# Expert stages of a decoder layer on one core: where expert rows and their fetches stand among the half blocks, and the order around the first value block

## The chip, the cores and the metric

One core of one Trainium2 chip. The metric is the device time of the whole kernel in microseconds (us), median of several runs. Engines: PE (TensorE, matmuls; PEld its weight loads), DVE (VectorE), ACT (ScalarE), POOL (GpSimd), SP (SyncE, issues most DMAs). HBM is the chip's memory, SBUF and PSUM the on-chip ones; PSUM has 8 banks of 512 float32 per partition.

## The reference, cut to what matters

The layer is a token mixer (two attention kinds) and then PEER, a channel mixer that picks 16 of 16384 experts per head and token. 16 meta tokens and 256 tokens; the width is 2048.

```
q = (t @ w_query).reshape(n_tok, 8, 2, 64)
s = einsum('thcd,hcnd->thcn', q, sub_keys)
v1, i1 = top_k(s[:, :, 0], 16);  v2, i2 = top_k(s[:, :, 1], 16)
best, j = top_k(v1[..., :, None] + v2[..., None, :], 16)     # over 256 sums
e_idx = i1[j // 16] * 128 + i2[j % 16];  gate = softmax(best)
a = gelu(einsum('cd,chkd->chk', t, expert_u[e_idx]))
out = einsum('chk,chkd->cd', gate * a, expert_v[e_idx])
```

## The kernel before, in words

The first part (norms, projections, attention, output, query) is not touched. It ends about 780 us after the start. Two expert stages follow, each with 128 blocks of 128 experts; a block of the tables is 1 MB. The first 192 tokens (TD) are computed densely: every expert is multiplied, and a table of gates, zero where an expert was not picked, weights the results. The last 64 tokens (TS) are computed from fetched rows: 8 heads x 16 experts for 64 tokens, 128 partitions at a time, are 64 fetches (ROWS) of `u` and later 64 of `v`, 1 MB each.

All products are float32 made from two parts: ACT rounds the 1 MB block to its high part (L457, `hi_block`), DVE subtracts to get the low part (L466/L468, `lo_block`), PE multiplies both. Time is counted in half blocks: DVE calls `step(m)` twice per block, and each step carries what the plan puts there.

**The u stage** (`expert_block`, 128 times). PE does 16 matmuls of 384 columns with the high part (L856) and 16 of 192 with the low part (L861), into bank 0, 1, 2 or 3 in turn. ACT copies half the bank out (L1221), DVE adds the other half for two blocks at once (`expert_sums`, L1777) and so frees the banks. In its steps DVE also does the routing (top 16 of each head, L1674 to L1714) and the products of fetched rows with the token (`row_product`, L1721, the tokens being in banks 4 to 7). The functions `row_at(n)`, `gather_at(n)` and `scatter_at(k)` say at which half block row n is used, and in which place of POOL's instruction order the fetch of row n and scatter k stand. POOL has no clock: it runs its instructions one after another, and waits only for what an instruction needs. Its list has 64 fetches (L1313) and 192 scatters of gates to the HBM table (L1318). There are 3 row buffers (RING), so the fetch of row n waits until row n-3 is used. After the last scatter POOL waits until all scatters are in HBM (L1351), then loads the gates of the first four blocks (L1353).

**SP** issues the load of block n+3 when the low part of block n is done: 3 buffers for the 1 MB blocks.

**The value stage** (`value_block`, 128 times, L879). 20 matmuls of 512 columns a block: 4 with the high part of the gated weights for the first 128 tokens (`part(0, j)`), 4 with their low part `Wlo`, 4 with `Wboth` for the other 64 (`part(1, j)`, banks 4 to 7), and 8 with the low part of the block. `part(0, 0)` writes banks 0 and 1, `part(0, 1)` banks 2 and 3. The weights come by a chain: DVE gates them (`gate_weights`, L1766), ACT rounds them (`weight_hi`, L1210 and L1211, once the block before the last is done on PE), DVE subtracts (`weight_lo`, L1771). DVE also sums the fetched `v` rows (`row_sum`, L1735), one in 3.7 half blocks.

Before, the first value block starts with a wait for banks 0 and 1, two matmuls, and a wait for the sum of the last two u blocks (banks 2 and 3), which DVE does for both at once after PE has ended block 127.

Of the kernel before, what the change touches and what calls it, by code (L numbers as in the profile page):

```python
# [29 lines left out]
ALU = mybir.AluOpType  # L30
# [3 lines left out]
P = 128  # L34
# [10 lines left out]
TD = 192  # L45
# [3 lines left out]
RING = 3  # L49
# [7 lines left out]
B_BRANCH, B_OUT, B_QUERY, B_U, B_V = KC, KC, HEADS, NK, NK  # L57
# [3 lines left out]
F_U = F_QUERY + B_QUERY  # L61
F_V = F_U + B_U
# [104 lines left out]
def hybrid_layer(nc, stream, u_cols, u_rows, v_rows, x_t, params, consts, h1_rows, gates_at, cum_at, out):  # L167
    with ExitStack() as ctx:
# [3 lines left out]
        def sem(name):  # L172
            return ctx.enter_context(nc.semaphore(name))
# [10 lines left out]
        psum = ctx.enter_context(nc.psum_tensor("psum", [P, 8 * 512], F32))  # L184

        def bank(b, a=0, w=512):
            return psum[:, b * 512 + a:b * 512 + a + w]
# [134 lines left out]
        W = arena[:, 0:NK * TD].rearrange("p (c t) -> p c t", c=NK)  # L322
# [12 lines left out]
        Whi = [xr[:, a:a + TD] for a in W_AT]  # L335
        Wlo = [xr[:, a + TD:a + 2 * TD] for a in W_AT]
        Wagain = [xr[:, a + 2 * TD:a + 2 * TD + TS] for a in W_AT]
        Wboth = [xr[:, a + TD + P:a + 2 * TD + TS] for a in W_AT]
# [6 lines left out]
        BEFORE = 12  # L345
# [4 lines left out]

        def row_at(n):
            if n < 46:
                return 6 + n * 9 // 2
            if n < ROWS:
                return 211 + (n - 46) * 5 // 2
            return 2 * B_U + 8 + (n - ROWS) * (2 * B_V - 20) // ROWS

        def gather_at(n):
            return max(row_at(n) - 8, row_at(n - RING) + 1) if n >= RING else -BEFORE

        def scatter_at(k):
            return k * 250 // (ROWS + NSEL) - 2
# [15 lines left out]
        U_BANKS = (0, 1, 2, 3)  # L378
# [5 lines left out]
        def f(ap):  # L384
            return ap.bitcast(F32)
# [4 lines left out]
        hi_done, lo_done, half_done = sem("hi_done"), sem("lo_done"), sem("half_multiplied")  # L390
        bank_free, upper_done = sem("bank_free"), sem("upper_products")
# [30 lines left out]
        low_part = sem("x_lo_products")  # L422
# [152 lines left out]
        def _(pe):  # L575
# [296 lines left out]
            def value_block(base, c, first, idle=None, residual=None):  # L872
                q = c % 2
                hi_w = whi[:, q * D:(q + 1) * D]

                def part(b, j, at, weights, low_part, begin, end):
                    for n in range(2):
                        src = lows[q][:, j, n * 512:(n + 1) * 512] if low_part else hi_w[:, (2 * j + n) * 512:(2 * j + n + 1) * 512]
                        last = mm(at[:, (b * 4 + j * 2 + n) * 512:(b * 4 + j * 2 + n + 1) * 512], weights, src,  # L879
                                  start=begin, stop=end, skip_group_check=True)  # L880
                    return last

                pe.wait_ge(w_hi, base + c + 1)
                pe.wait_ge(hi_done, base * 2 + 2 * F_V + 2 * c + 2)
                if first:
                    pe.wait_ge(bank_free, F_V)
                part(0, 0, psum, Whi[q][:, 0:P], False, first, False)
                if first:
                    pe.wait_ge(bank_free, 2 + F_V)
                part(0, 1, psum, Whi[q][:, 0:P], False, first, False)  # L890
                pe.wait_ge(w_lo, base + c + 1)
                if first:
                    pe.wait_ge(row_used, ROWS)
                if residual is None:
                    for j in range(2):
                        part(0, j, psum, Wlo[q][:, 0:P], False, False, False)
                        part(1, j, psum, Wboth[q], False, first, False)
                else:
                    part(0, 0, psum, Wlo[q][:, 0:P], False, False, False)
                    part(0, 1, psum, Wlo[q][:, 0:P], False, False, False)  # L900
                    part(1, 1 - residual, psum, Wboth[q], False, False, False)
                    pe.wait_ge(low_residual, residual + 1)
                    part(1, residual, psum, Wboth[q], False, False, False)
                pe.wait_ge(lo_done, base * 2 + 2 * F_V + 2 * c + 2)
                for j in range(2):
                    last = part(1, j, psum[0:TS, :], Whi[q][:, P:TD], True, False, True)
                    if j == idle:
                        last.then_inc(low_bank_idle, 1)
                for j in range(2):
                    part(0, j, psum, Whi[q][:, 0:P], True, False, True).then_inc(half_done, 1)  # L910

            value_block(0, 0, True)
            value_block(0, 1, False)
            with pe.Fori(0, B_V // 2 - 4) as i:
                for q in range(2):
# [444 lines left out]
        def _(dve):  # L1360
            V = nc.vector
# [266 lines left out]
            for k in range(KC):  # L1628
                q = k % 2
# [86 lines left out]
            def row_product(n):  # L1716
                s = row_buffer(n)
                if n == 0:
                    dve.wait_ge(x_rows_ps, 1)
                dve.wait_ge(row_in[s], row_loads(n))  # L1720
                V.tensor_tensor_reduce(out=got[s], in0=x_rows, in1=got[s], scale=1.0, scalar=0.0, op0=ALU.mult,  # L1721
                                       op1=ALU.add, accum_out=dots[:, n:n + 1]).then_inc(row_used, 1)
# [14 lines left out]
            def step(m):  # L1737
                for t, k in ROUTE_STEPS.get(m, ()):
                    route(t, k)
                if m in GATE_STEPS:  # L1740
                    route(GATE_STEPS[m], 8)
                if m in ROW_STEPS:
                    n = ROW_STEPS[m]
                    if n < ROWS:
                        row_product(n)
                    else:
                        row_sum(n)

            dve.nop().then_inc(sc_taken, 1)
            for k in range(2 * B_QUERY):  # L1750
# [3 lines left out]
                if k % 2:  # L1754
                    q = k // 2
# [4 lines left out]
            def gate_weights(chunk):  # L1760
                n, q = chunk // 2 % 2, chunk % 2
                if chunk < 4:
                    dve.wait_ge(first_gates[n], 16)
                else:
                    dve.wait_ge(gates_in[n], 16 * (chunk // 4))
                V.tensor_tensor(W[:, chunk, :], W[:, chunk, :], gate_in[n][:, q * TD:(q + 1) * TD], ALU.mult).then_inc(scaled, 1)  # L1766

            def weight_lo(chunk):
                q = chunk % 2
                dve.wait_ge(w_hi, chunk + 1)  # L1770
                V.tensor_tensor(Wlo[q], W[:, chunk, :], f(Whi[q]), ALU.subtract).then_inc(w_lo, 1)  # L1771

            def expert_sums(n):
                dve.wait_ge(half_done, 2 * F_U + 2 * n + 4)
                dve.wait_ge(low_part, n + 2)
                both = psum[:, U_BANKS[n % 4] * 512:(U_BANKS[n % 4] + 2) * 512].rearrange("p (b t) -> p b t", b=2)
                V.tensor_tensor(W[:, n:n + 2, :], both[:, :, 0:TD], W[:, n:n + 2, :], ALU.add).then_inc(bank_free, 2)  # L1777

            for n in range(B_U):
                if n and n % 2 == 0:  # L1780
                    expert_sums(n - 2)
                step(2 * n)
                step(2 * n + 1)
                if n < B_U - 1:
                    lo_block(dve, n + 1)
                if n == B_U - 2:
                    gate_weights(0)
            weight_lo(0)
            expert_sums(B_U - 2)
            lo_block(dve, B_U)  # L1790
            gate_weights(1)
            def bank_residual(n):
# [3 lines left out]

            for c in range(B_V):
                n = B_U + c
                step(2 * n)
                if c < B_V - 2:  # L1800
                    gate_weights(c + 2)
                step(2 * n + 1)
                if c == B_V - 2:
                    bank_residual(0)
                if c < B_V - 1:
                    weight_lo(c + 1)
                if c < B_V - 2:
                    lo_block(dve, n + 1)
                if c == B_V - 2:
                    for z in range(2):  # L1810
                        last_lo_half(dve, z)
                if c in (B_V - 5, B_V - 4):
                    half = slice((c - B_V + 5) * HALF, (c - B_V + 6) * HALF)
                    rows_at = psum[0:TS, 2048 + half.start:2048 + half.stop]
                    dve.wait_ge(rows_back[1], 16)
                    dve.wait_ge(low_bank_idle, c - B_V + 6)
                    V.tensor_tensor(rows_at, rows_at, h1_high[0:TS, half], ALU.add).then_inc(low_residual, 1)
                if c == B_V - 6:
                    dve.wait_ge(acc_moved, 16)
                    V.tensor_tensor(res[TS:P, :], res[TS:P, :], acc[TS:P, :], ALU.add).then_inc(sparse_out, 1)  # L1820
# [81 lines left out]
```

## Time and profile before

| | us |
|---|---|
| median of 3 runs | 1981.13 (1979.11 to 1982.59) |
| the profiled execution | 1977.39 |
| its span, first to last instruction | 1975.5 |
| PE busy | 1950.1 (99% of the span) |
| DVE busy | 1682.3 (85%) |
| ACT busy | 1120.6 (57%) |
| POOL busy | 726.9 (37%), almost all of it in the u stage |

TensorE's granted clock was 0.999 over the span. A PE row counts as busy while its matmuls are in flight, so the share says that PE had work nearly all the time; the gaps between blocks show in the timeline and in the sums over stretches. The two expert stages together run from 781.9 us to the end, 60% of the span.

### The profile page before, as it was taken

The numbers are of one execution on the slowest core, as the hardware profiler recorded it, in microseconds if no ns is written. First come the engines' busy times: TensorE is split into PE (matmuls) and PEld (weight loads), VectorE is DVE, ScalarE is ACT, GpSimd is POOL, SyncE is SP. The second block draws the span as 40 slices with busy tenths as digits, with TensorE's granted clock in tenths as the row PEclk, the third lists the DMA queues.
The fourth block names the chain that finished last, engine by engine and source line by source line (L and its number), as shares of the span: only waits on it lengthen the run. The fifth ranks groups of instructions, "written<-read, shape, count | busy, mean of one in ns | idle before, by whom it ended". The sixth has DMA issues, their size and how long they took to land. (4 is left out here: it accounts for less than half of the span.)

```text
span 1975.5 us, 32460 instructions
## 1 busy us (share of the span) xinstructions
PE 1950.1 (99%) x11696; PEld 1734.8 (88%) x11696; DVE 1682.3 (85%) x2366; ACT 1120.6 (57%) x1585; POOL 726.9 (37%) x406
## 2 busy tenths in 40 slices
PE   8999999999999999999999999999999999999999
PEld 7899989998888888999999999999777777777776
DVE  6877778776878777999999999989888888888897
ACT  7565556555676455666565655645555555555454
POOL 0301110111000001888888888886222232222220
PEclk9999999999999999999999999999999999999999
DMA  5756654566455556999999999999999999999997
GB/s 215 255 168 197 196 191 161 190 202 199 152 175 187 182 188 224 323 312 328 320 323 337 331 307 335 326 383 404 343 379 379 363 374 383 378 375 376 371 385 256
DMA packets 137574, 566.48 MB, mean 287 GB/s; under 512 B 44008, under 2 KB 52080, under 8 KB 88112
## 3 DMA queue, kind: packets, MB, share of 16 engines
q1 hardware_dynamic: 87456, 415.09, 58.5%
q0 software_dynamic: 49776, 148.44, 22.2%
q10 hardware_dynamic: 288, 2.36, 0.3%
q8 instruction: 17, 0.28, 0.1%
q14 instruction: 37, 0.30, 0.0%
HBM read 548.30 MB, written 16.88 MB: 286 GB/s over the span
## 5 line engine op out<-in xcount | busy, mean ns | idle before, releaser
L451 DVE TENSOR_TENSOR wlo<-raw,whi 128x1024 fp32r<-128x1024 f32 x242 | 295.9, 1231 | 112.4 <-PE psum L606 72.1
L856 PE MATMUL psum<-xr,whi 128*128 128x384 f32 x2048 | 381.0, 337 | 2.1 <-ACT whi L457 2.1
L879 PE MATMUL psum<-whi,xr 128*128 128x512 f32 x1512 | 364.0, 389 | 0.8 <-DVE arena L1777 0.6
L856 PEld LDWEIGHTS psum<-xr,whi 128*128 128x128 f32 x2048 | 351.1, 188 | 2.9 <-ACT whi L457 2.6
L602 PE MATMUL psum<-xr,whi 128*128 128x512 f32 x1312 | 336.1, 398 | 5.1 <-issue 3.7
L879 PEld LDWEIGHTS psum<-whi,xr 128*128 128x128 f32 x1512 | 283.4, 188 | 62.4 <-DVE arena L1777 1.1
L457 ACT ACTIVATE whi<-raw 128x2048 fp32r<-128x2048 f32 x168 | 320.8, 1910 | 27.3 <-DMA raw<-v_rows 14.2
L444 ACT ACTIVATE whi<-raw 128x1024 fp32r<-128x1024 f32 x244 | 249.9, 1053 | 101.3 <-DMA raw<-stream 44.2
L1313 POOL DMA_INDIRECT arena<-v_rows,small x64 | 143.8, 2246 | 400.2 <-DVE arena L1735 397.9
L602 PEld LDWEIGHTS psum<-xr,whi 128*128 128x128 f32 x1312 | 236.1, 189 | 50.7 <-issue 4.4
L1318 POOL DMA_INDIRECT gates<-arena x96 | 219.9, 2290 | 29.3 <-issue 28.9
L1318 POOL DMA_INDIRECT gates<-small x96 | 197.3, 2055 | 29.3 <-issue 29.0
L468 DVE TENSOR_TENSOR wlo<-raw,whi 128x2048 fp32r<-128x2048 f32 x76 | 173.8, 2287 | 26.3 <-issue 25.8
L1210 ACT ACTIVATE xr<-arena 128x192 fp32r<-128x192 f32 x128 | 46.7, 365 | 260.4 <-PE psum L879 256.7
L606 PEld LDWEIGHTS psum<-xr,wlo 128*128 128x128 f32 x1312 | 177.9, 189 | 13.8
L1313 POOL DMA_INDIRECT arena<-u_rows,small x64 | 92.3, 1442 | 260.5 <-DMA small<-arena 240.9
L468 DVE TENSOR_TENSOR xr<-raw,whi 128x2048 fp32r<-128x2048 f32 x77 | 176.2, 2289 | 12.4 <-issue 11.4
L606 PE MATMUL psum<-xr,wlo 128*128 128x256 f32 x1312 | 181.8, 281 | 0.0
L1303 POOL TENSOR_TENSOR arena<-arena 128x256 f32<-128x256 f32 x32 | 23.7, 741 | 416.9 <-DVE arena L1450 416.9
L457 ACT ACTIVATE whi<-arena 128x2048 fp32r<-128x2048 f32 x85 | 162.3, 1910 | 15.9 <-DMA arena<-u_cols 9.9
L1221 ACT ACTIVATE arena<-psum 128x192 f32<-128x192 f32 x128 | 42.5, 332 | 222.4 <-PE psum L861 222.4
L1721 DVE CUSTOM_DVE_ANT_0 arena<-psum,arena 128x2048 f32<-128x2048 f32 x64 | 146.2, 2284 | 12.5 <-DMA arena<-u_rows,small 11.7
(276 smaller groups left out, 3232.2 us busy)
## 6 DMA issues: line engine op xcount, KB each, us to landing
raw<-stream SPq DMA_DIRECT2D x244, 512.0 KB, 3.3
raw<-v_rows SPq DMA_DIRECT2D x85, 1024.0 KB, 7.6
raw<-u_cols SPq DMA_DIRECT2D x84, 1024.0 KB, 6.3
arena<-v_rows SPq DMA_DIRECT2D x43, 1024.0 KB, 7.8
arena<-u_cols SPq DMA_DIRECT2D x42, 1024.0 KB, 5.7
gates<-arena POOLq DMA_DIRECT2D x8, 1536.0 KB, 9.7
small<-gates SPq DMA_DIRECT2D x62, 192.0 KB, 8.2
arena<-x_t SPq DMA_DIRECT2D x4, 544.0 KB, 5.9
```

The costliest lines, as they stand in the source:

```text
L444: nc.scalar.activation(whi[:, s * HALF:(s + 1) * HALF], raw[:, s * HALF:(s + 1) * HALF], ACT.Copy).then_inc(hi_done, 1)
L451: nc.vector.tensor_tensor(wlo[:, k % 2 * HALF:(k % 2 + 1) * HALF], raw[:, s * HALF:(s + 1) * HALF], f(whi[:, s * HALF:(s + 1) * HALF]), AL ...
L457: nc.scalar.activation(whi[:, b % 2 * D:(b % 2 + 1) * D], slots[b % 3], ACT.Copy).then_inc(hi_done, 2)
L468: nc.vector.tensor_tensor(lows[b % 2], *halves, ALU.subtract).then_inc(lo_done, 2)
L602: mm(bank(b), whi[:, s * HALF + c * P:s * HALF + (c + 1) * P], both[c], start=start and c == 0, stop=False)
L606: last = mm(bank(b, 0, T), wlo[:, s * HALF + c * P:s * HALF + (c + 1) * P], hi[c], start=False, stop=stop and c == 7)
L856: mm(bank(at, 0, 2 * TD), hi_w[:, c * P:(c + 1) * P], z_all[:, :, c, 0:TD // TS, :], start=c == 0, stop=False)
L879: last = mm(at[:, (b * 4 + j * 2 + n) * 512:(b * 4 + j * 2 + n + 1) * 512], weights, src, start=begin, stop=end, skip_group_check=True)
L1210: A(Whi[q], one_weight(chunk), ACT.Copy)
L1313: pool.indirect_dma_start(got[s], None, table, bass.IndirectOffsetOnAxis(sparse_row[:, h:h + 1].bitcast(U32), 0)).then_inc(row_in[s], 16)
L1318: pool.indirect_dma_start(every, bass.IndirectOffsetOnAxis(at.bitcast(U32), 0), gate, None, compute_op=ALU.add).then_inc(scattered[b], 16)
L1721: V.tensor_tensor_reduce(out=got[s], in0=x_rows, in1=got[s], scale=1.0, scalar=0.0, op0=ALU.mult, op1=ALU.add, accum_out=dots[:, n:n + 1]) ...
```

## The change

- `row_at`: rows 0 to 45 of `u` stand 4.4 half blocks apart (before 4.5), rows 46 to 63 start at half block 207 and stand 2.7 apart (before 211 and 2.5).
- `gather_at`: the fetch of row n stands one half block after the use of row n-3, and no longer at the later one of that place and 8 half blocks before its own use.
- The first value block: banks 2 and 3 are written last. Before the wait for them now stand the high and low weights on banks 0 and 1 and the four products on banks 4 to 7.
- The sums of u blocks 126 and 127 are made singly (`expert_sum`), that of 126 before the steps of block 127.
- In the value stage `weight_lo` stands ahead of the steps (row sums) of its block.

```
         def row_at(n):
             if n < 46:
-                return 6 + n * 9 // 2
+                return 6 + n * 22 // 5
             if n < ROWS:
-                return 211 + (n - 46) * 5 // 2
+                return 207 + (n - 46) * 27 // 10
...
         def gather_at(n):
-            return max(row_at(n) - 8, row_at(n - RING) + 1) if n >= RING else -BEFORE
+            return row_at(n - RING) + 1 if n >= RING else -BEFORE
...
                 part(0, 0, psum, Whi[q][:, 0:P], False, first, False)
-                if first:
-                    pe.wait_ge(bank_free, 2 + F_V)
-                part(0, 1, psum, Whi[q][:, 0:P], False, first, False)
+                if not first:
+                    part(0, 1, psum, Whi[q][:, 0:P], False, False, False)
                 pe.wait_ge(w_lo, base + c + 1)
                 if first:
+                    part(0, 0, psum, Wlo[q][:, 0:P], False, False, False)
                     pe.wait_ge(row_used, ROWS)
-                if residual is None:
+                    for j in range(2):
+                        part(1, j, psum, Wboth[q], False, True, False)
+                    pe.wait_ge(bank_free, 2 + F_V)
+                    for weights in (Whi[q], Wlo[q]):
+                        part(0, 1, psum, weights[:, 0:P], False, weights is Whi[q], False)
+                elif residual is None:
...
+            def expert_sum(n):
+                dve.wait_ge(half_done, 2 * F_U + 2 * n + 2)
+                dve.wait_ge(low_part, n + 1)
+                V.tensor_tensor(W[:, n, :], bank(U_BANKS[n % 4], 0, TD), W[:, n, :], ALU.add).then_inc(bank_free, 1)
...
             for n in range(B_U):
                 if n and n % 2 == 0:
                     expert_sums(n - 2)
+                if n == B_U - 1:
+                    expert_sum(n - 1)
                 step(2 * n)
...
             weight_lo(0)
-            expert_sums(B_U - 2)
+            expert_sum(B_U - 1)
             lo_block(dve, B_U)
...
             for c in range(B_V):
                 n = B_U + c
+                if c < B_V - 1:
+                    weight_lo(c + 1)
                 step(2 * n)
                 if c < B_V - 2:
                     gate_weights(c + 2)
                 step(2 * n + 1)
                 if c == B_V - 2:
                     bank_residual(0)
-                if c < B_V - 1:
-                    weight_lo(c + 1)
```

## Rows read from the trace of the kernel before

**Rows 1.** Busy time by stretch: us (instructions) per engine, clock, DMA share, GB/s.

```profile
core 0: us, PE busy (x) PEld busy (x) DVE busy (x) ACT busy (x) POOL busy (x), PEclk, DMA share, GB/s
781.90:1266.00 484.10, 480.51 (x3336) 474.98 (x3335) 469.85 (x835) 291.39 (x346) 422.30 (x203) 1.00 0.95 325
1266.00:1383.40 117.40, 112.76 (x773) 110.44 (x772) 104.67 (x105) 61.60 (x67) 89.38 (x56) 1.00 1.04 386
1383.40:1943.00 559.60, 558.59 (x2442) 431.36 (x2441) 490.10 (x435) 287.10 (x369) 140.65 (x62) 1.00 0.97 371
```

**Rows 2.** PE in order of time: start us, us, engine, line, shapes, count.

```profile
796.53 2.97 PE L856 MATMUL psum<-xr,whi 128*128 128x384 f32 x16
...
801.10 2.97 PE L856 MATMUL psum<-xr,whi 128*128 128x384 f32 x16
...
1383.40 0.64 PE L879 MATMUL psum<-whi,xr 128*128 128x512 f32 x2
1384.67 2.57 PE L879 MATMUL psum<-whi,xr 128*128 128x512 f32 x10 [0.63 <-DVE arena L1777]
...
1388.92 2.89 PE L879 MATMUL psum<-whi,xr 128*128 128x512 f32 x12
...
1408.45 2.10 PE L879 MATMUL psum<-whi,xr 128*128 128x512 f32 x8 [0.19 <-DVE xr L1771]
```

**Rows 3.** Waits, 781.9 to 1383.4: total us, times, longest us.

```profile
DVE arena L1721 <- DMA arena<-u_rows,small: 11.7, 6, 2.8
...
PEld psum L861 <- DVE xr L468: 4.4, 9, 0.8
...
POOL arena L1313 <- DVE small L1721: 3.7, 5, 2.1
```

**Rows 4.** POOL by line, 775 to 1375: busy us, mean ns, idle before.

```profile
L1318 POOL DMA_INDIRECT gates<-arena x96 | 219.9, 2290 | 29.3 <-issue 28.9 <-DVE small L1721 0.3
L1318 POOL DMA_INDIRECT gates<-small x96 | 197.3, 2055 | 29.3 <-issue 29.0 <-DMA gates<-arena 0.3
L1313 POOL DMA_INDIRECT arena<-u_rows,small x64 | 92.3, 1442 | 260.5 <-DMA small<-arena 240.9 <-issue 18.0 <-DVE small L1721 1.7
```

**Rows 5.** POOL in order of time; L1318 are scatters, L1313 fetches.

```profile
800.27 3.32 POOL L1318 DMA_INDIRECT gates<-small  x1 [0.30 <-issue]
...
1248.24 3.60 POOL L1318 DMA_INDIRECT gates<-small  x1 [0.30 <-issue]
...
1260.86 1.57 POOL L1318 DMA_INDIRECT gates<-small  x1 [0.30 <-issue]
...
1363.51 1.56 POOL L1318 DMA_INDIRECT gates<-small  x1 [0.30 <-issue]
1365.37 1.75 POOL L1313 DMA_INDIRECT arena<-u_rows,small  x1 [0.30 <-issue]
1374.39 1.21 POOL L1353 DMA_DIRECT2D small<-gates  x2 [7.28 <-DMA gates<-small]
```

**Rows 6.** Landing of L1313 before and after 1260, then of L1353.

```profile
DMA to landing us min/median/max: 5.6/6.9/10.7
...
DMA to landing us min/median/max: 6.1/11.1/15.0
...
DMA to landing us min/median/max: 4.7/4.7/4.8
```

**Rows 7.** DVE in order of time.

```profile
799.88 2.29 DVE L468 TENSOR_TENSOR wlo<-raw,whi 128x2048 fp32r<-128x2048 f32 x1
...
1161.95 2.29 DVE L1721 CUSTOM_DVE_ANT_0 arena<-psum,arena 128x2048 f32<-128x2048 f32 x1 [2.85 <-DMA arena<-u_rows,small]
...
1281.29 2.28 DVE L1721 CUSTOM_DVE_ANT_0 arena<-psum,arena 128x2048 f32<-128x2048 f32 x1
...
1381.29 0.35 DVE L1766 TENSOR_TENSOR arena<-arena,small 128x192 f32<-128x192 f32 x1
...
1384.54 2.28 DVE L468 TENSOR_TENSOR wlo<-arena,whi 128x2048 fp32r<-128x2048 f32 x1
```

**Rows 8.** ACT in order of time, the end of the first rounded weights.

```profile
1381.95 0.24 ACT L1211 ACTIVATE xr<-arena 128x64 fp32r<-128x64 f32 x1
```

More of the change, by code:

```diff
@@ L887, in value_block @@
                 part(0, 0, psum, Whi[q][:, 0:P], False, first, False)
-                if first:
-                    pe.wait_ge(bank_free, 2 + F_V)
-                part(0, 1, psum, Whi[q][:, 0:P], False, first, False)
+                if not first:
+                    part(0, 1, psum, Whi[q][:, 0:P], False, False, False)
                 pe.wait_ge(w_lo, base + c + 1)
                 if first:
+                    part(0, 0, psum, Wlo[q][:, 0:P], False, False, False)
                     pe.wait_ge(row_used, ROWS)
-                if residual is None:
+                    for j in range(2):
[4 more added lines that the diff above has]
+                elif residual is None:
                     for j in range(2):
                         part(0, j, psum, Wlo[q][:, 0:P], False, False, False)
-                        part(1, j, psum, Wboth[q], False, first, False)
+                        part(1, j, psum, Wboth[q], False, False, False)
                 else:
```

## The prediction

> **What bounds the kernel now.** I read the sums by stretch first [rows 1]. From 781.9 to 1383.4 (the u stage) PE is busy nearly all of the time, but so are DVE (469.9 of 484.1 us in the first part, 104.7 of 117.4 in the last) and POOL (422.3 of 484.1). In the value stage PE is alone: 558.6 of 559.6, DVE 490.1. So the value stage has little to give, and the u stage has three engines near their limit.
>
> PE's timeline gives the pace of a u block: 801.10 - 796.53 = 4.57 us, a half block 2.29 [rows 2]. 128 blocks make 585.3; the stage takes 1383.4 - 781.9 = 601.5. PE loses 16.2 us there, 0.7 of it to a score product that belongs to the first block. The waits [rows 3] say for whom: for the low parts of DVE, in small pieces. DVE itself stands 11.7 us in 6 waits for fetched rows that haven't landed. The reader should see that DVE hardly ever waits for PE here: it is DVE's work plus its waits that fill the stage.
>
> Third, POOL by line [rows 4]: 219.9 + 197.3 + 92.3 = 509.5 us of instructions and 76 us of 0.3 us gaps, together 585.5, in an unbroken run from about 779.5 to 1365.37 + 1.75 = 1367.1 [rows 5]. POOL waits for data some 2 us in it. So the fetches come late because POOL is late, and what ends the u stage also hangs on POOL: after the last scatter (ends 1363.51 + 1.56 = 1365.1) it waits till 1374.4 for the table to be whole, the loads issued there land 4.8 later [rows 6], at 1379.2, DVE gates the weights at 1381.29 [rows 7], ACT has them rounded at 1382.2 [rows 8], and PE starts the value stage at 1383.40 [rows 2], when its last u block is done. From landing to rounded weights the chain needs 0.1 + 0.35 + 0.55 = 1.0 us, so POOL would let the value stage start at 1380.2. **At most 3.2 us can be won at the end of the u stage unless POOL itself ends sooner.**
>
> **The change part by part.**
>
> *Rows at 4.4, fetches once a buffer is free.* No instruction is added or removed: 64 fetches, 192 scatters, 64 products. Counting the plan, fetch 35 has 115 scatters ahead of it instead of 121, fetch 46 153 instead of 158, fetches 47 to 61 mostly 2 to 4 fewer. A scatter and its gap are 417.2 / 192 + 0.3 = 2.47 us [rows 4].
>
> Row 35: it waited 2.85 us [rows 7]. Its fetch is 6 scatters (15 us) earlier, its use 3 half blocks (6.9 us at most) earlier: 8 us of gain against a wait of 2.85. Gone. Fetch 46 now stands where scatter 153 began, at 1248.24 [rows 5], plus one fetch (1.3): 1249.5. That is 16 us earlier, and its wait of 2.1 goes too.
>
> Then it comes back. Fetch 47 has 156 scatters ahead; POOL started scatter 156 at 1260.86 with 46 fetches done [rows 5], one more makes 1262.2. DVE comes to row 47 at half block 209 instead of 213. Of a half block 1.8 us are work other than rows (2.29 less 2.2 / 4.5), so it comes 4 x 1.8 = 7.2 earlier, and 4.9 earlier by the two waits gone: 1281.29 - 12.1 = 1269.2 [rows 7]. A fetch took 6.1 to 15.0 to land there, median 11.1 [rows 6]: 1262.2 + 10 = 1272, a wait of about 3 us. Laying all late rows this way, DVE's waits fall from 11.7 to about 9 (2 to 18 for a POOL 2% faster or slower, since 2% of 587 is 12 us). DVE and with it PE end the u stage about 3 us earlier, near 1380.4. Row 63 is used at half block 252 instead of 253, and 2.7 instead of 2.5 apart eases the stretch in which the DMA share is 1.04 [rows 1]; I leave both in the 3 us.
>
> Does POOL now wait more? Fetch 3 stands 7 scatters in, at 800.27 [rows 5], and row 0 is used at 799.88 [rows 7]: no wait. Fetch 4 waits perhaps 0.5. Later POOL lags behind the free buffers by 3 us and more. So POOL ends where it did, 1367.1, within 0.5. But its last instructions change places: fetch 63 had all 192 scatters ahead and has 190 now. The last scatter ends last, at 1367.1 instead of 1365.1, with 1 MB of rows just issued ahead of it. The table is whole 2.0 us later or more (all else equal 1376.4; if it waits for that megabyte, up to 1379). Gates land at 1381.2, weights are rounded at 1382.2, up to 1384.8. I take 1382.7, nearer the lower end, as the wait of before (9.3 us) already had fetch 62 ahead of it. **Value stage starts 0.7 us earlier** (bounds: 3.2 earlier, 1.4 later).
>
> In sentences apart: the Trainium skill, in "DMA: Bandwidth & Descriptors", section "Queues, rings and completion order", says that on each DMA engine descriptors are consumed in ring order. Rows 5 agree (7.28 us of wait, with the scatters behind a fetch), and by that rule the two last scatters land behind fetch 63; this is what the slower rival below is made of.
>
> *POOL's pace.* A scatter took 1.56 at best and 3.32 or 3.60 at worst [rows 5]. The one of 3.32 began 0.4 us after DVE's L468 at 799.88, and ended 1.4 after that instruction [rows 7]. The mean is 2.17, so 0.6 x 192 = 117 us of POOL's run is time behind DVE instructions. The change shifts rows against low parts, hence which scatters meet which instruction. Nothing favours a sign; five stretches of about 33 scatters would have to move together. Estimate: 4 us either way on POOL's end. The skill ("SBUF — State Buffer", section "SBUF: two separate sides") has it as a lock: a DVE instruction with two SBUF inputs and a GpSimd one exclude each other, whoever comes first. By that rule filling DVE's idle time with low parts slows POOL, which speaks against this change; 3 us less idle at the present share would cost POOL well under 1 us.
>
> *First value block.* Its pitch was 1388.92 - 1383.40 = 5.52, 0.95 over the normal 4.57, with 0.63 of it in the wait for banks 2 and 3 [rows 2]. That wait goes behind 8 matmuls (1.8 us) and costs nothing. Next late is the block's low part: DVE began it at 1384.54 [rows 7] and PE wants it after 12 matmuls, 2.75 us in. In the new order DVE has, after the rounded weights, `weight_lo` (0.35), one single sum (about 0.35) and the low part (2.28): 3.05. PE stalls 0.3 to 0.4. **0.6 us won** (bounds 0 and 0.95). The early sum of block 126 adds one DVE instruction (under 0.3) in a place where DVE waits for gates anyway.
>
> *weight_lo ahead of row sums.* It matters where PE waited for it: 0.19 at 1408.45 [rows 2], where the accumulator is cleared and the sums start. But the low part of the block behind it in DVE's queue isn't earlier, as DVE has the same work; the stall moves from the fifth matmul to the thirteenth. 0.1 won. Elsewhere `weight_lo` now may wait for ACT's rounding, which follows PE's end of a block by 0.6 us, and behind it wait the row sum, the next gates (ACT), the low part (PE) and with it SP's next load. DVE idles 69.5 us in 559.6 [rows 1], 0.55 a block, so a loss of 0.3 in blocks with a row is covered in most. **Cost 0.2** (0 to 1).
>
> Sum: -0.7 - 0.6 - 0.1 + 0.2 = -1.2 us. The profiled execution would take 1977.39 - 1.2 = 1976.2 (span 1974.3 and 1.9 around it). It lay 3.7 below the median of the runs shown, 1981.13; the same step from the median gives **1979.9**.
>
> **The rivals.**
>
> *All waits for rows go (faster).* If POOL comes out 4 to 6 us faster in the new interleaving, fetches land in time, the 11.7 us of DVE's waits vanish and PE ends the u stage by 1376. The last scatter, 2.0 later by its new place, still ends 2 to 4 earlier, gates land at 1377.2 to 1375.2, and the value stage starts 1.0 later, 5.2 to 7.2 earlier than before. With the 0.5 of the value stage: 1981.1 - 6.7 = 1974.4. For it: fetches do stand up to 6 scatters earlier, and the late stretch is less dense. Against: POOL's total is unchanged, and an earlier use undoes the earlier fetch. Chance 0.31, smaller gains beyond 4 us included.
>
> *The table of gates comes later (slower).* The last scatters land behind the megabyte of fetch 63, and POOL loses a few us in its locks. From a table whole later than 1383.4 - 1.0 - 4.8 = 1377.6 the value stage starts later than before; with POOL 4 later, 2.0 for the new place and 2.6 for the megabyte, it starts at 1388.8, 5.4 later, less 0.5: 1986.0. Against: POOL would need bad luck besides the order. Chance 0.17.
>
> *Nothing moves.* DVE's 3 us are won and the gates' chain gives them back: 1981. This differs from my forecast by less than can be told; both together 0.52.
>
> **How the numbers follow.** A change under 0.2% (4 us) can't be told from none here. Faster 0.31, same 0.52, slower 0.17. The range leaves out some 1 in 10 at each end: POOL's 4 us and the rivals' times give 1973.5 to 1986.
>
> **What would show it.** Right: row 35 without a wait; DVE's total for rows about 9 and now on rows 47 to 52 and 59; POOL's run about 587 us, its wait before L1353 still 7 us or more, gates landing 1381 to 1382; the wait before the first value block's third matmul gone, one of 0.3 at its thirteenth. Wrong: POOL's run shorter than 583 or longer than 591, DVE waits for rows near 0, or new gaps in value blocks with a row sum.

## The result, and the profile after

| | median us | runs | ratio to before, 95% interval |
|---|---|---|---|
| before | 1981.13 | 11 (one of them 3189.65, left out of the ratio) | |
| after | 1986.68 (1977.04 to 1988.83) | 11 | 1.0027 (1.0014 to 1.0039) |

The change makes the kernel slower by some 5.5 us. The forecast was 1979.9 with 1973.5 to 1986.0 and only 0.17 on slower. Note the lowest of the 11 runs after: 1977.04, six microseconds below the next one. It is taken up again with e6.

The profiled execution took 1988.83. First the sums over the part of the u stage to half block 210, the rest of it, and the value stage's main part, as in [rows 1].

```profile
784.40:1268.50 484.10, 479.12 (x3315) 473.75 (x3314) 469.37 (x835) 290.64 (x345) 421.98 (x201) 1.00 0.94 325
1268.50:1391.57 123.07, 118.44 (x793) 115.90 (x792) 105.92 (x106) 61.81 (x69) 94.97 (x59) 0.97 1.00 364
1391.57:1951.00 559.43, 555.61 (x2427) 428.49 (x2426) 491.03 (x432) 283.44 (x369) 185.13 (x62) 1.00 0.94 370
```

The u stage lasts 1391.57 - 784.40 = 607.2 us, 5.7 more than before. That is the size of the slowdown. Two other differences of this one execution are no part of it: the untouched first part took 2.5 us longer (784.4 against 781.9), and the value stage 3.2 longer (595.3 against 592.1). The version with the row and fetch edits alone (e1 below) had 591.9 there, and was as slow. Here are the sums over the whole u stage, after and then before.

```profile
784.40:1391.57 607.17, 597.56 (x4107) 589.66 (x4105) 575.29 (x940) 352.46 (x413) 516.94 (x259) 0.99 0.95 333
```

```profile
781.90:1383.40 601.50, 593.27 (x4107) 585.42 (x4105) 574.52 (x939) 352.99 (x413) 511.67 (x259) 1.00 0.97 337
```

Of the 5.7 us PE is busy for 4.3 more with the same 4107 matmuls (half clock, shown below), and idle for 1.4 more. DVE has hardly more work (469.4 + 105.9 against 469.9 + 104.7 us), so its waits are read next, 784.4 to 1391.6, as in [rows 3].

```profile
DVE arena L1726 <- DMA arena<-u_rows,small: 15.0, 7, 4.9
...
PEld psum L861 <- DVE xr L468: 7.1, 9, 3.0
...
POOL arena L1318 <- DVE small L1726: 2.6, 5, 0.9
```

DVE's waits for rows have grown from 11.7 to 15.0 us. Row 35 waits no more, but row 38 does (2.5), and of the late rows above all 46 (1.5), 49 (4.9), 52 (3.5) and 61 (1.4). The longest wait of PE's weight loads for a low part is 3.0 us (before 1.9). Now POOL by line, as in [rows 4].

```profile
L1323 POOL DMA_INDIRECT gates<-arena x96 | 208.3, 2169 | 29.3 <-issue 29.3
L1323 POOL DMA_INDIRECT gates<-small x96 | 199.2, 2075 | 29.3 <-issue 29.0 <-DVE small L1726 0.3
L1318 POOL DMA_INDIRECT arena<-u_rows,small x64 | 107.7, 1683 | 263.8 <-DMA small<-arena 243.4 <-issue 17.5 <-DVE small L1726 2.6
```

The scatters take 407.5 us (before 417.2), the fetches 107.7 (92.3): the same 256 instructions 5.7 us more, plus 0.9 us more of waits for a free buffer (2.6 + 0.3 against 1.7 + 0.3). POOL's run, from its first fetch to the end of its last scatter or fetch, is 594.1 us, before 587.6. The fetches are longer as a kind, and so is their landing: first the line for the first 46 after, with duration min/median/max, and their landing; then the same two lines of before.

```profile
L1318 POOL DMA_INDIRECT arena<-u_rows,small x46: 937/1846/3075, 782.0 to 1249.5; - x46
...
DMA to landing us min/median/max: 5.4/9.3/10.7
```

```profile
L1313 POOL DMA_INDIRECT arena<-u_rows,small x46: 937/1002/3073, 779.5 to 1259.6; - x46
...
DMA to landing us min/median/max: 5.6/6.9/10.7
```

The wait of row 38 and what it does, PE in order of time, then DVE.

```profile
1187.30 1.92 PE L861 MATMUL psum<-xr,wlo 128*128 128x192 f32 x16
1189.06 2.98 PE L856 MATMUL psum<-xr,whi 128*128 128x384 f32 x16
1194.74 2.77 PE L861 MATMUL psum<-xr 128*128 128x192 f32 x16 [2.71 <-DVE xr L468]
1197.31 3.88 PE L856 MATMUL psum<-xr,whi 128*128 128x384 f32 x16
```

```profile
1190.19 2.29 DVE L1726 CUSTOM_DVE_ANT_0 arena<-psum,arena 128x2048 f32<-128x2048 f32 x1 [2.49 <-DMA arena<-u_rows,small]
...
1192.40 2.29 DVE L468 TENSOR_TENSOR xr<-raw,whi 128x2048 fp32r<-128x2048 f32 x1
...
1296.11 2.29 DVE L1726 CUSTOM_DVE_ANT_0 arena<-psum,arena 128x2048 f32<-128x2048 f32 x1 [4.87 <-DMA arena<-u_rows,small]
```

DVE stands 2.49 us for the row; the low part of the block, queued behind it, starts that much later, and PE stands 2.71. The reader should then look at the groups after 1194.74: 2.77 us for 16 matmuls that take 1.92 otherwise, 3.88 instead of 2.97. The granted clock says why; these are short stretches around it, columns as in [rows 1].

```profile
1192.38:1195.79 3.41, 1.04 (x9) 1.05 (x10) 3.33 (x9) 0.00 (x0) 3.17 (x1) 1.00 0.81 259
1195.80:1199.00 3.20, 3.20 (x15) 3.20 (x15) 3.11 (x4) 1.45 (x2) 2.90 (x2) 0.50 0.98 376
```

Behind the idle time PE got half its clock, 1.2 GHz, for 3.41 us. That costs (2.77 - 1.92) + (3.88 - 2.97) = 1.8 us more. Two more such pieces lie at 1284.6 and 1301.6, 2 to 3 us behind stalls of PE of 1.98 and 1.40 us; before had stalls of up to 1.6 in the u stage and no such piece. Half clock isn't the whole of it: one run of after took 1985.15 us with a granted clock of 0.999 over its span, which is that of the profile before.

The end of the stage: POOL, PE and ACT in order of time, as in [rows 5], [rows 2] and [rows 8].

```profile
1373.62 2.50 POOL L1323 DMA_INDIRECT gates<-small  x1 [0.30 <-issue]
1385.87 1.23 POOL L1358 DMA_DIRECT2D small<-gates  x2 [9.76 <-DMA gates<-small]
```

```profile
1389.81 1.92 PE L861 MATMUL psum<-xr 128*128 128x192 f32 x16
1391.57 2.93 PE L879 MATMUL psum<-whi,xr 128*128 128x512 f32 x12
1394.81 2.06 PE L879 MATMUL psum<-wlo,xr 128*64 128x512 f32 x8 [0.31 <-DVE wlo L468]
1396.71 2.88 PE L879 MATMUL psum<-whi,xr 128*128 128x512 f32 x12
```

```profile
1389.89 0.24 ACT L1216 ACTIVATE xr<-arena 128x64 fp32r<-128x64 f32 x1
```

The table is whole 9.76 us after the last scatter (before 9.3, where fetch 63 was issued behind all scatters). The first weights are rounded at 1390.1, and PE starts the value stage at 1391.57, right behind its last u block. So the gates were not what came last. PE's own u blocks were. The first value block takes 1396.71 - 1391.57 = 5.14 us (5.52 before), with the 0.31 us stall at its thirteenth matmul.

### The profile page after: what moved, and what is told of

Its sections match the earlier page's. It is cut to its first block, busy times and chain, and to the rows that moved or that the text cites. A ratio compares the mean times of both kernels' runs of the same rounds, so it can differ in the third digit from the quotient of the medians.

```text
span 1986.9 us, 32462 instructions
## 1 busy us (share of the span) xinstructions
PE 1955.9 (98%) x11696; PEld 1740.2 (88%) x11696; DVE 1687.2 (85%) x2367; ACT 1118.0 (56%) x1585; POOL 776.8 (39%) x406
## 4 chain that ended last, share of the span: by engine, by line
PE 31%; POOL 11%; issue 3%; DVE 2%; DMA 2%; ACT 1%; DVEq 0%; POOLq 0%; ACTq 0%
PE psum L879 26%; POOL gates L1323 9%; PE psum L856 3%; PE psum L861 2%; POOL arena L1318 2%; DMA arena<-v_rows 1%; DVE xr L468 1%; DVE wlo L468 0%; DMA raw<-v_rows 0%; PE psum L933 0%; ACT whi L457 0%; DMA arena<-u_rows,small 0%; DMA gates<-arena 0%; DVE arena L1726 0%; DVE arena L1740 0%
## 5 line engine op out<-in xcount | busy, mean ns | idle before, releaser
L1318 POOL DMA_INDIRECT arena<-v_rows,small x64 | 187.7, 2933 | 359.0 <-DVE arena L1740 358.4
L1323 POOL DMA_INDIRECT gates<-arena x96 | 208.3, 2169 | 29.3 <-issue 29.3
L1318 POOL DMA_INDIRECT arena<-u_rows,small x64 | 107.7, 1683 | 263.8 <-DMA small<-arena 243.4
```

The source lines that it names most:

```text
L1318: pool.indirect_dma_start(got[s], None, table, bass.IndirectOffsetOnAxis(sparse_row[:, h:h + 1].bitcast(U32), 0)).then_inc(row_in[s], 16)
L1323: pool.indirect_dma_start(every, bass.IndirectOffsetOnAxis(at.bitcast(U32), 0), gate, None, compute_op=ALU.add).then_inc(scattered[b], 16)
```

## The experiments

Ratios are to the kernel before, run beside each on the same chip, with 95% intervals; each kernel had 5 to 12 timed runs. "Row waits" are DVE's waits for fetched rows in the u stage of the one profiled execution.

### Which part of the change: e1 to e6

e1 has the first two edits of the diff (rows and fetches), e2 only the move of `weight_lo`, e3 only the first value block with its single sums, e4 only the fetch rule, e5 only the rows. e6 is e1 with the late rows left at their old place:

```
 def row_at(n):
-    return 6 + n * 9 // 2                     # n < 46
+    return 6 + n * 22 // 5                    # e1, e5, e6
-    return 211 + (n - 46) * 5 // 2            # n < 64
+    return 207 + (n - 46) * 27 // 10          # e1, e5
 def gather_at(n):
-    return max(row_at(n) - 8, row_at(n - RING) + 1) if n >= RING else -BEFORE
+    return row_at(n - RING) + 1 if n >= RING else -BEFORE     # e1, e4, e6
```

> Kernel before with the new places of rows and fetches only (4.4 and 2.7 half blocks, fetch once the buffer is free). Theory P (the u stage costs: POOL's run gets longer, table of gates whole 9 us later): 4 to 6 us slower than before, u stage 605 to 608 us, value stage as before. Theory V (the cost is weight_lo ahead of the row sums): within 1.5 us of before. Theory C (the difference is PE's clock, granted at half for 3.4 us now and then): follows the number of such dips in the profile and not the code, 0 to 8 us.

> Kernel before with weight_lo ahead of the row sums only. Theory V: 2 to 4 us slower, stalls at value blocks 5 and 14 to 17, slack of the low part in blocks with a row sum down from 1.95 to 1.45 us. Theory P: within 1 us of before, u stage as before. My forecast on record gave this edit 0.1 us.

> Kernel before with the new order of the first value block and the single sums only. By all theories 0.3 to 0.6 us faster: pitch of value block 0 5.1 us instead of 5.52. Not to be told from no change in the time, but in the profile.

> Kernel before with the fetch places only (once the buffer is free), rows where they were. Fetches 5 to 6 scatters earlier against unchanged uses: by my forecast's picture the waits for rows 35 and 46 go and the late ones stay, DVE's waits 11.7 to 7, 0 to 3 us faster. By theory P as a matter of the order in POOL's queue alone (a fetch beside a scatter, last scatters behind fetch 63) 4 to 6 us slower, POOL's run over 590 us.

> Kernel before with the new places of the rows (4.4, then 207 and 2.7) and the old rule for the fetches. What is known: rows and fetches together made it 0.25% slower and POOL's run 592.7 us, fetches alone left both (586.1 us). Theory S (the spacing of 4.4 sets rows and low parts so that POOL's instructions meet longer DVE ones; its run gets some 6 us longer, and rows and gates wait for it): POOL's run 591 us or more, 3 to 6 us slower. Theory I (only rows and fetches together): within 1.5 us of before, POOL's run 585 to 588.

> Rows 0 to 45 at 4.4 half blocks and the new fetch rule; rows 46 to 63 where they were before (from 211, 2.5 apart). Theory S: as slow as rows and fetches together (3 to 6 us), a wait for row 38 and half-rate clock behind it, as the early part is the same. Rival L (the late rows, spread and begun earlier, cost): within 1.5 us of before.

| | median us | ratio | row waits us | u stage us | POOL's run us |
|---|---|---|---|---|---|
| e1 rows + fetches | 1986.11 | 1.0025 (1.0010 to 1.0039) | 12.0 | 606.1 | 592.7 |
| e2 weight_lo | 1981.43 | 1.0003 (0.9990 to 1.0016) | 9.3 | 599.2 | 584.7 |
| e3 first block | 1979.50 | 0.9999 (0.9988 to 1.0010) | 9.7 | 598.6 | 584.5 |
| e4 fetches | 1980.06 | 1.0007 (0.9996 to 1.0018) | 11.3 | 598.9 | 586.1 |
| e5 rows | 1978.62 | 0.9993 (0.9980 to 1.0006) | 7.7 | 599.2 | 584.9 |
| e6 early rows + fetches | 1987.67 | 1.0035 (1.0022 to 1.0047) | 7.1 | 599.0 | 584.7 |

e1 is the whole slowdown. The two edits at the value stage are nothing that can be told from none. Neither the rows nor the fetch rule is slow alone: it takes both, and of the rows only the early ones. In e4 row 35's wait went as expected, but row 46's stayed (2.2), and DVE's waits came to 11.3 and not to 7. e2 and e3 leave POOL's code alone, and still its run was 584.7 and 584.5 where before had 587.6: 3 us are within what one code does.

e6 is the puzzle and the key. Its median is 1987.67, its seven runs 1978.13, 1984.90, 1986.03 and on to 1992.11, and the profiled execution is that of 1978.13. A run near 1977 stands alone in after (1977.04) and e1 (1977.01) too. Up to row 45 the three have the same instructions in the u stage. So one code goes two ways, and profiles of the two courses can be laid side by side. First after, POOL and then DVE; then e6, the same; then e1 (the profiled execution is that of 1982.63, with a wait at row 38).

```profile
1068.58 3.50 POOL L1323 DMA_INDIRECT gates<-arena  x1 [0.30 <-issue]
1072.39 2.58 POOL L1318 DMA_INDIRECT arena<-u_rows,small  x1 [0.30 <-issue]
```

```profile
1068.38 2.27 DVE L468 TENSOR_TENSOR xr<-raw,whi 128x2048 fp32r<-128x2048 f32 x1
```

```profile
1068.38 1.56 POOL L1318 DMA_INDIRECT gates<-arena  x1 [0.30 <-issue]
1070.25 1.38 POOL L1313 DMA_INDIRECT arena<-u_rows,small  x1 [0.31 <-issue]
```

```profile
1068.48 2.27 DVE L468 TENSOR_TENSOR xr<-raw,whi 128x2048 fp32r<-128x2048 f32 x1
```

```profile
1066.68 3.50 POOL L1318 DMA_INDIRECT gates<-arena  x1 [0.30 <-issue]
1070.49 2.58 POOL L1313 DMA_INDIRECT arena<-u_rows,small  x1 [0.30 <-issue]
```

```profile
1066.48 2.27 DVE L468 TENSOR_TENSOR xr<-raw,whi 128x2048 fp32r<-128x2048 f32 x1
```

The three u stages start at 784.40, 784.49 and 782.75. In after the low part begins at 1068.38 and the scatter 0.20 later: it takes 3.50 us, until 1.4 after the low part. In e6 the scatter begins 0.10 **ahead** of the low part and takes 1.56. The low part takes 2.27 either way. A shift of 0.3 us in who comes first has become 1.9 us on POOL. In e1 POOL comes to this scatter as early in its stage as in e6 (within 0.04 us), but DVE begins the low part 0.26 earlier: the scatter again begins 0.20 behind it and takes 3.50. After had got its 0.28 us on POOL long before, at a scatter of 3.52 us at 867.46 that took 3.26 in e6. From fetch 28, the one behind the scatter, to fetch 38 the same 44 instructions take 1180.51 - 1072.39 = 108.1 us in after, 1178.61 - 1070.49 = 108.1 in e1, and 1171.77 - 1070.25 = 101.5 in e6. POOL is then 8.7 us late, row 38 waits 2.5, the clock halves, and late rows follow. In e6 row 38 did not wait.

That low parts do this can be counted in the trace of after. Of the 192 scatters of the u stage 94 began while a low part was running; they took 1.56 to 3.66 us, and half of them ended 1.43 us or more after it. The 98 others took 1.55 to 1.88, among them 59 that began during a row product, which has one of its inputs in PSUM (1.56 to 1.59). Of the 64 fetches 36 began in a low part (0.99 to 3.08 us), the 28 others took 0.94 to 1.00. Before, it was 100 scatters and 29 fetches. Why most times of this code belong to the slow course and few to the other isn't shown.

The Trainium skill has this rule in "SBUF — State Buffer", section "SBUF: two separate sides": of a DVE instruction with two SBUF inputs and a GpSimd one that reads SBUF, "whichever" starts first has the shared port pair for its whole instruction. The rows above agree on POOL's side. On DVE's side they don't: in e6 the scatter was first, and the low part behind it took 2.27 us as always.

### Does POOL's lateness carry it: e10, e11

```
+            LEFT_OUT = (73, 74, 75, 76)          # e10, in the changed kernel
+                        if n in LEFT_OUT:
+                            continue
```

```
+                        if n == 84:              # e11, in the kernel before: ahead of scatter 84
+                            pool.wait_ge(row_used, 25)
```

> The changed kernel with 4 of the 192 scatters left out (numbers 73 to 76, just ahead of fetch 24), so 512 gates are missing in the table; DVE, ACT and PE have all their work. POOL comes 9 to 10 us earlier to fetch 24 and everything behind it. Theory (the slowdown passes through POOL's lateness): the wait at row 38 goes, with it PE's stall and the 3.4 us of half clock behind it; the waits for late rows fall from 9 to 10 us to under 3; gates land some 8 us earlier; 1977 (1973 to 1980), at or below the kernel before. Rival (the loss is made elsewhere: DMA traffic or DVE's order): 1984 or more.

> The kernel before, with one wait added: POOL holds scatter 84 until row 24 is used, which stops it for some 10 us at 257 us into the u stage; no work is added. Theory (POOL's lateness at fetches 28 to 38 is the cause, whatever makes it): waits at rows 28 to 40, above all at 35 (2.9 us before), grow by several us, PE stalls behind one of them, the u stage takes 5 to 10 us longer and the whole 1985 to 1990. Rival (POOL's place does not matter by itself, the changed kernel loses by its new interleaving with the low parts): within 2.5 us of the kernel before.

e10 took 1978.46, ratio 0.9990 (0.9979 to 1.0001): some 8 us below the changed kernel, for 10 us less of POOL. e11 took 1989.55, ratio 1.0048 (1.0034 to 1.0062): 8 us above before, with no work added. Both came out as the theory said in size. In place e11 did so in part, and its profile is that of the fastest of its five runs (1984.91, u stage 607.5 us): most of its loss is one wait, of row 25 (7.3 us), behind which PE stood 7.1 us. The clock was at half for 6.8 us, the last 3.7 of them after PE had begun again. Row 34 waited 2.2, row 35 not at all. These are its waits and the added one, then what e10's waits became.

```profile
DVE arena L1723 <- DMA arena<-u_rows,small: 16.8, 8, 7.3
POOL gates L1318 <- DVE small L1723: 11.3, 2, 11.0
```

```profile
DVE arena L1729 <- DMA arena<-u_rows,small: 6.1, 3, 2.6
```

In e10 row 38 doesn't wait, the u stage takes 600.2 us, and the only piece of half clock in it lies at 1318; the late waits fell to 6.1, not under 3 as expected. So lateness of POOL by itself was worth most of its own length here (some 8 us for 10 to 11). e10 also changes which instructions meet, so alone it doesn't tell lateness from meetings; e11 makes POOL late by a wait, and gives the other direction. How much of e11's 8 us went through row 25 alone and how much through the rows behind, this run doesn't tell apart.

### A rule or a meeting: e9, e13, e14

```
-    return 6 + n * 22 // 5                   # of the changed kernel, n < 46
+    return 6 + n * 9 // 2                    # e9
+    return 7 + n * 22 // 5                   # e14
-    return row_at(n - RING) + 1 if n >= RING else -BEFORE
+    return row_at(n - RING) + 2 if n >= RING else -BEFORE     # e13
```

> The changed kernel with one line put back: rows 0 to 45 again 4.5 half blocks apart; everything else of the change stays. Theory (it is the pair of closer early rows and earlier fetches that puts POOL some 7 to 9 us behind): no difference to the kernel before, 1980 (1977 to 1983), ratio within 0.2%, no wait at row 38, no second of half clock near 1195. Rival (the late rows' new places together with the new fetch rule, or the two edits at the value stage, carry it): 1985 to 1987 as the changed kernel, gates landing over 600 us after the u stage's start.

> The changed kernel with each fetch two half blocks after the use of row n-3 instead of one, so that one or no scatter more stands ahead of it. Theory of the meeting (which scatter or fetch starts inside a low part decides, and the pattern around fetches 26 to 28 is particular to one placing): POOL does not fall 9 us behind there; the time leaves 1986.7 by 4 us or more, to 1976 to 1982, or a new lateness shows elsewhere. Rival (early rows at 4.4 with fetches ahead of their old place always cost this): 1984 to 1989, and with fetches one scatter later the wait at row 38 grows by 2 us.

> The changed kernel with rows 0 to 45 one half block later (7 + 4.4 n), and their fetches with them; the late rows stay. Theory of the meeting: as DVE's rows fall into the other half of each block, the pattern of meetings is a new one: 1976 to 1982, or late at another place. Rival (spacing and fetch rule cost it by themselves): 1984 to 1989, POOL late at fetches 28 to 38 again.

e9: 1984.26, ratio 1.0017 (1.0006 to 1.0028). The wait at row 38 and the half clock there are gone, as expected, but it has made a fault of its own: row 45 falls on half block 208 and row 46 on 207, ahead of it. That row waits 8.46 us. The time lies between the two expected ones and says nothing on whether the pair of early edits is needed; e4, e5 and e6 are the clean form of the question.

e13: 1986.51, ratio 1.0030 (1.0017 to 1.0042). Here the rival was right in the time: a scatter more ahead of each fetch changes nothing in the median. Its runs part again, three from 1976.4 to 1979.9 and nine from 1984.6 to 1989.1, and its profiled execution belongs to the three (1977.6: row waits 5.6 us, POOL's run 582.5), so whether row 38 waits longer in the nine isn't shown.

e14: **1977.44, ratio 0.9984 (0.9976 to 0.9993)**; all 11 runs between 1973.7 and 1980.4. One half block, with spacing and fetch rule as in the changed kernel, is worth 9 us. Its waits and fetches:

```profile
DVE arena L1726 <- DMA arena<-u_rows,small: 9.5, 5, 3.1
```

```profile
L1318 POOL DMA_INDIRECT arena<-u_rows,small x64 | 106.0, 1657 | 260.2 <-DMA small<-arena 241.0 <-issue 17.4 <-DVE small L1726 1.8
```

The fetches are as long as in after (106.0 us), but the scatters take 401.2 instead of 407.5, fetch 38 is issued 390.3 us into the stage instead of 396.1, row 38 finds its row there, and DVE's waits are 9.5: the number forecast for the change. So early fetches at 4.4 don't cost this by rule. The edit has a second effect: rows 0 to 45 are used 2.3 us later, and that alone nearly covers row 38's wait of 2.5. But row 46 stands where it did, with as many scatters ahead of its fetch, and this fetch is issued 471.5 us into the stage instead of 480.6. So POOL's pace changed too. The loss belongs to one placing of rows against low parts, in which most runs are slow (10 of the 11 of after took over 1983 us).

### Shorter low parts: e7, e8, e12, e15

If POOL is held by whole low parts, halves should let it in sooner. The kernel has halves in its last 24 u blocks (L466).

```
-        LO_SPLIT = B_U - 24
+        LO_SPLIT = B_U - 64                   # e7, e15; e8 in the changed kernel; e12: B_U - 96
```

e12 and e15 have the changed kernel's first value block too.

> Kernel before with the low parts of the last 64 u blocks subtracted in halves (before: the last 24), 40 more DVE instructions. Theory B (POOL's pace behind DVE's long two-input instructions is what bounds the u stage): a scatter among the split blocks takes 1.8 us instead of 2.3, some 45 scatters gain 20 us, DVE's 12 us of waits for rows go, table of gates whole 15 us earlier, 4 to 9 us faster, less 3 us for DVE's added instructions (0.06 us each). Rival D (DVE's own load bounds it): 2 to 3 us slower.

> Changed kernel with the same split of the last 64 u blocks. Theory B: POOL's disadvantage no longer matters, within 1.5 us of the split kernel with the old plan, so 4 to 9 us faster than the changed one. Rival D: slower than the changed kernel by 2 to 3 us.

> The kernel before with the low parts of the last 96 u blocks (before: 24) made as two halves, and the changed kernel's order around the first value block. With the last 64 in halves alone it took 0.9964 of the kernel before. Theory (shorter DVE instructions let POOL in sooner): POOL gets still more spare time, but row waits were already at 1.6 us; 0.4 us from the first value block; 1973 (1970 to 1976). Rival (POOL no longer bounds and 32 more split instructions cost DVE 0.05 to 0.1 us each, 2 to 3 us where DVE is full of routing): 1976.

> The kernel before with the low parts of the last 64 u blocks as two halves and the changed kernel's order around the first value block. Theory (the two are independent, halves 0.9964, the order 0.4 us): 1973 (1971 to 1976). Rival (the order takes something back, as in the version with 96 blocks at 0.9989): 1977 or more.

| | median us | ratio | row waits us | u stage us |
|---|---|---|---|---|
| e7 before, 64 in halves | 1973.72 | 0.9964 (0.9951 to 0.9977) | 0.9 | 595.4 |
| e8 after, 64 in halves | 1977.11 | 0.9985 (0.9974 to 0.9996) | none | 598.3 |
| e15 e7 + first block | 1976.38 | 0.9980 (0.9966 to 0.9993) | 2.5 | 595.0 |
| e12 96 + first block | 1978.23 | 0.9989 (0.9977 to 1.0002) | 0.9 | 596.0 |

e7 in its profiled execution, POOL's scatters and fetches:

```profile
L1318 POOL DMA_INDIRECT gates<-arena x96 | 200.5, 2088 | 29.2 <-issue 29.2
L1318 POOL DMA_INDIRECT gates<-small x96 | 186.3, 1941 | 29.3 <-issue 29.3
L1313 POOL DMA_INDIRECT arena<-u_rows,small x64 | 89.8, 1403 | 288.6 <-DMA small<-arena 242.4 <-DVE small L1721 30.1 <-issue 16.1
```

The scatters fell from 417.2 to 386.8 us, and POOL now waits 30.1 us for free row buffers: it is no longer what is late. e7 is faster than both kernels, by 7 us against before. e15 and e7 can't be told apart (their intervals overlap), nor can e12 and e15, which differ by 96 halves against 64 alone; e12's 1978.23 was above both of its expectations, e15's lay between its two. e8 shows that with POOL at ease the changed kernel loses its disadvantage against before. It was expected within 1.5 us of e7 and came out 3.4 above, with intervals that just touch; that rest is open.

## Why the prediction was wrong

**The step that failed** is "POOL's pace", and with it "POOL ends where it did, 1367.1, within 0.5". The prediction worked out that 117 us of POOL's run is time behind DVE instructions, then took it as an average over many meetings: "Nothing favours a sign; five stretches of about 33 scatters would have to move together". They can move together: POOL has no clock of its own, one lost race put it 1.9 us later, and the next ones are met from there. Its run came out at 594.1 us, above the 591 that the text had set as the mark of being wrong and beyond its 4 us either way, and fetch 38 comes 8.7 us later than in the other course of the same code. The 117 us were also of scatters alone. The fetches are held as well, and it is they that grew (92.3 to 107.7 us), while the scatters shrank by 9.7.

In the sum this is the term "-0.7", the value stage starting earlier: the u stage came out 5.7 us longer. The forecast had fetch 47 issued at 1262.2, 480.3 us into the stage, and its row used 487.3 in; in after it was 488.9 and 494.5. Where POOL is on time the working holds: in e14 fetch 47 is issued at 479.3. The average over placings was perhaps right (e14 faster, after slower, e4 and e5 the same); the spread was not, and it was the outcome.

**DVE's waits, "from 11.7 to about 9"**: 15.0. Row 35's wait went as worked out, and the waits returned at rows 46 to 61. With POOL on time the figure is near (e14 9.5, e5 7.7, e6 7.1). The text's own band for a POOL 2% slower reached 18, so this is the same error and not another.

**What a wait costs** was missing. A DVE wait was priced at its own length. The one of 2.5 us had a second price, the 1.8 us of half clock behind PE's stall; not every stall has it, as the list at the end shows.

**Who comes last at the end of the stage**: the forecast had the table of gates as the bound and as its slower rival. It gave a fair time (1986.0 for 1986.68) by luck, from the wrong place. The parts of that chain were right: the table was whole 9.76 us behind the last scatter where the lower end of 9.3 was taken, so fetch 63's megabyte cost 0.4 and not 2.6 (with the same order 9.36 in e1 and 10.09 in e5). Such small differences don't show that the scatters waited for the megabyte at all. But the weights were rounded 1.4 us before PE asked.

**First value block, 0.6 won**: 0.38 (and 5.14 us in e3's profile as in after's), with the stall of 0.31 in the place and size given. Right, and too small to be timed (e3). **weight_lo, 0.1 won and 0.2 lost**: nothing measured (e2). **"Fetch 4 waits perhaps 0.5"**: POOL's waits for free buffers, 2.6 us in 5 with the usual gap of 0.3 in each, come to 1.1: small, and nearly right.

**The chances.** Slower had 0.17 for one mechanism. The mechanism that the text itself named as unsigned deserved its own case, with "POOL is late and stays late" on the slow side, at a price of about its length.

## What to carry to other kernels

An engine that runs a fixed list with no clock, and whose instructions are long or short by who comes first, is not priced by its mean: ask how late it can become and who then waits, and give both signs their chance. Where that is the pace maker, a shift of the work by half a block is a cheap variant to time (here 9 us against the changed kernel, 3 against before), and so is shortening what it meets (halves instead of whole instructions, 7 us against before). When the times of one code fall in two groups, look for a profile of each: the first instruction after which they part, and don't come together again, points at the cause.

## What the runs showed of the hardware

- A scatter issued by GpSimd took 1.56 us when it began 0.10 us before a DVE instruction with two SBUF inputs and 3.50 when it began 0.20 after. That instruction took 2.27 both times. Scatters that began during a row product, with one input in PSUM, took 1.56 to 1.59 (59 of them in after).
- Behind or within stalls of PE TensorE's clock was granted at half, 1.2 GHz: for 3.41 us behind 2.71 (1.8 us of time lost), for 6.83 with stalls of 7.1 and 7.6 (e11, e9), where it fell before the stall was over. Stalls between 1.2 and 2.3 us had a piece behind them in some places (after, 1.40 and 1.98) and none in others (before, 1.62; after in the value stage, 1.68). No run here isolates the condition.
- After and e5 have two pieces of half clock in the untouched first part, at 540 and 731 us, and before has none there (one at 9 us, where after has none); their u stages start 2.5 and 3.2 us later. Single profiles of kernels with the same code there differ by that much.
